# Attention: the next head's hi and lo parts in thirds over three blocks, on ScalarE and VectorE; modulation semaphores cleared

## What is computed

```python
# 8 heads, 2048 queries, 2304 keys (2048 tokens and 256 of context), q and k 96 wide, v 64 wide
def one_block(qblk):
    s = jnp.einsum('bqhd,bkhd->bhqk', qblk, k).astype(jnp.float32) * scale
    p = jax.nn.softmax(s, axis=-1).astype(v.dtype)
    return jnp.einsum('bhqk,bkhd->bqhd', p, v)
```

## Time and profile before

| | us |
|---|---|
| timed runs, median of 3 | 3417.44 (3409.56 to 3417.75) |
| the profiled execution, its own time | 3412.3 |
| its span | 3410.5 |
| TensorE busy over the span | 3076.6 (90%) |
| VectorE busy | 1947.3 (57%) |
| ScalarE busy | 1375.1 (40%) |
| GpSimd busy | 648.5 (19%) |
| attention stage, about | 1094 to 2116 |

### The profile page before, as it was taken

How to read it: one execution, slowest core, us unless ns; L and a number is a source line. 1 busy time by engine, 2 the same in 40 slices (tenths; PEclk the granted TensorE clock), 3 DMA queues, 4 the chain that set the end, 5 groups by cost and what they waited for, 6 DMA issues and landing times. The chain is left out here.

```text
span 3410.5 us, 43961 instructions
## 1 busy us (share of the span) xinstructions
PE 3076.6 (90%) x14693; PEld 2177.3 (64%) x14693; DVE 1947.3 (57%) x2632; ACT 1375.1 (40%) x2061; POOL 648.5 (19%) x459
## 2 busy tenths in 40 slices
PE   6799999999886899999999997998399999999992
PEld 1355555555586565565565563777298989989892
DVE  1133333333475677777777775444766666766663
ACT  0133333333222655666566664211244444444432
POOL 0011111111254233223322321211011111101011
PEclk9899999999877899999999998999599999999996
DMA  8521121111223110110110101332366667676656
GB/s 320 149 70 61 62 68 61 61 61 55 99 82 80 23 24 12 32 32 5 31 32 5 32 5 55 139 108 105 122 198 208 211 205 229 203 216 201 212 159 234
DMA packets 254709, 363.74 MB, mean 107 GB/s; under 512 B 36436, under 2 KB 170583, under 8 KB 252888
## 3 DMA queue, kind: packets, MB, share of 16 engines
q1 hardware_dynamic: 245336, 327.97, 30.0%
q0 software_dynamic: 9216, 33.56, 4.4%
HBM read 279.65 MB, written 81.83 MB: 106 GB/s over the span
## 5 line engine op out<-in xcount | busy, mean ns | idle before, releaser
L467 PE MATMUL bank<-w_in_sb,h_T 128*128 128x512 f32 (+1 forms) x1440 | 609.3, 578 | 2.1 <-DVE h_T L616 2.1
L1643 PE MATMUL ebank<-gathered_T,w_gate_up 128*128 128x256 f32 x4608 | 555.6, 282 | 3.5 <-DVE gathered_T L1836 1.7
L1643 PEld LDWEIGHTS ebank<-gathered_T,w_gate_up 128*128 128x128 f32 x4608 | 550.9, 189 | 7.5 <-issue 6.3
L1077 PE MATMUL abank<-scores,head_v 128*128 128x512 f32 x1152 | 546.2, 602 | 2.2 <-ACT scores L1115 2.2
L1040 PE MATMUL abank<-head_qT,head_kT 96*128 96x512 f32 x1728 | 504.8, 437 | 24.5 <-POOL head_qT L1019 24.5
L467 PEld LDWEIGHTS bank<-w_in_sb,h_T 128*128 128x128 f32 x1440 | 270.1, 191 | 299.0 <-issue 298.8
L1040 PEld LDWEIGHTS abank<-head_qT,head_kT 96*128 96x128 f32 x1728 | 327.5, 190 | 172.1 <-issue 96.1
L1103 ACT ACTIVATE scores<-abank 128x512 f32<-128x512 f32 x576 | 314.3, 608 | 77.0 <-PE abank L1040 71.2
L1077 PEld LDWEIGHTS abank<-scores,head_v 128*128 128x128 f32 x1152 | 218.3, 194 | 180.7 <-issue 163.2
L1026 POOL TENSOR_TENSOR scores<-scores,max_for_pool 128x1536 f32<-128x1536 f32 x64 | 220.9, 3474 | 571.3 <-ACT max_for_pool L1109 571.3
L1115 ACT ACTIVATE scores<-scores 128x1536 f32<-128x1536 f32 x192 | 287.4, 1498 | 40.0 <-DVE scores L1157 35.6
(11 more groups left out here) (258 smaller groups left out, 3470.2 us busy)
## 6 DMA issues: line engine op xcount, KB each, us to landing
w_gate_up_whole<-in_w_exp_gate SPq DMA_DIRECT2D x48, 1024.0 KB, 5.4
w_gate_up_whole<-in_w_exp_up SPq DMA_DIRECT2D x48, 1024.0 KB, 8.0
w_down_whole<-in_w_exp_down SPq DMA_DIRECT2D x192, 256.0 KB, 3.6
ada_w<-in_w_ada SPq DMA_DIRECT2D x12, 2048.0 KB, 12.6
scratch_ret<-ret_rows SPq DMA_DIRECT2D x72, 256.0 KB, 2.5
x_tile<-in_x_all SPq DMA_DIRECT2D x18, 512.0 KB
w_in_sb<-in_w_in SPq DMA_DIRECT2D x4, 2048.0 KB, 18.8
chunk_qk<-scratch_ret SPq DMA_DIRECT2D x16, 512.0 KB
```

The source lines that it names most:

```text
L467: m = pe.matmul(banks[bank][:, 0:n], hT[u][:, k, :], w_in[:, k, lo:lo + n], start=(k == 0), stop=(k == KD - 1))
L1077: m = pe.matmul(banks[5 + j % 2][:, :], v1[u][:, kt, :], sc[j % 2][:, kt, :], start=(kt == 0), stop=(kt == T - 1))
L1643: x = pe.matmul(banks[f % 3][:, j * CAP:(j + 1) * CAP], w_gu[c][:, wp, j, k, o:o + P], xsT[:, xp, k, :], start=(k == 0 and n == 0), stop=( ...
```

## The change

- `split_next` on ScalarE and VectorE instead of ScalarE and GpSimd. A head's 2304 key columns and 2048 query columns are cut at 768 and 1536. Piece n of both is prepared in turn n (turns 0, 1, 2) for the pair's second head and in turn 4 + n (4, 5, 6) for the next pair's first head.
- ScalarE rounds a piece of k and of q after its six groups; VectorE subtracts the same pieces after the block's output, at the end of its turn. GpSimd has no part in it.
- `rounded` and `rest` count six steps a head. `head_ready` still waits for all of them.
- Head 0 is prepared in the same thirds, all subtractions on VectorE.
- Keys and queries have one loaded-semaphore and values another. For head 0 TensorE waits for the parts alone and for values only after the first scores.
- The modulation stage allocates its semaphores itself, has GpSimd clear them at its end, and an empty block (a barrier) follows.

```diff
@@ modulation
-    with ExitStack() as ctx:
+    with stage_semaphores(nc) as sem, ExitStack() as ctx:
...
+    yield sem
+    nc.clear_and_free_semaphores(taken)
+    with nc.Block():
+        pass
@@ attention
-        kv_loaded = ParitySignal(nc, ctx, "head_kv_loaded", 4)
+        kq_loaded, v_loaded = ParitySignal(nc, ctx, "head_kq_loaded", 3), ParitySignal(nc, ctx, "head_v_loaded")
+        THIRD = TOK // 3
+        def thirds(u, n):
+
+            c = slice(n * THIRD, (n + 1) * THIRD)
+            return (kT[u], k_whole[u], c), (qT[u], q_whole[u], slice(c.start, min(c.stop, SEQ)))
+
         def split_next(split, pair, j):
 
-            if j == 1:
-                split(pair * 2 + 1, 1)
-            if j == 5 and not (isinstance(pair, int) and pair == H // 2 - 1):
-                split(pair * 2 + 2, 0)
+            if j < 3:
+                split(pair * 2 + 1, 1, j)
+            if 4 <= j < 7 and not (isinstance(pair, int) and pair == H // 2 - 1):
+                split(pair * 2 + 2, 0, j - 4)
@@ gpsimd
-            def split(head, u, parts=(0, 1)):
-
-                for n in parts:
-                    x, whole = ((kT[u], k_whole[u]), (qT[u], q_whole[u]))[n]
-                    sg["rounded"].wait(pool, head, n + 1)
-                    pool.tensor_tensor(x[:, 1, :], whole[:, 1, :], x[:, 0, :].bitcast(F32), ALU.subtract).then_inc(sg["rest"].sem, 1)
...
-                split_next(split, pair, j)
-
-            split(0, 0, parts=(1,))
@@ tensor
             def head_ready(head, u):
-                kv_loaded.wait(pe, head, u)
+                kq_loaded.wait(pe, head, u)
+                v_loaded.wait(pe, head, u)
                 sg["rounded"].wait(pe, head)
                 sg["rest"].wait(pe, head)
...
-            pe.wait_ge(ones_set, 2)
-            head_ready(0, 0)
+            sg["rounded"].wait(pe, 0)
+            sg["rest"].wait(pe, 0)
             for kt in range(T):
                 score(0, 0, 0, kt)
             max_rows(0)
             max_spread(0)
+            pe.wait_ge(ones_set, 2)
+            v_loaded.wait(pe, 0, 0)
@@ scalar
+            def split(head, u, n):
+
+                kq_loaded.wait(act, head, u)
+                for x, whole, c in thirds(u, n):
+                    act.activation(x[:, 0, c], whole[:, 1, c], ACT.Copy).then_inc(sg["rounded"].sem, 1)
@@ vector
+            def split(head, u, n):
+
+                for i, (x, whole, c) in enumerate(thirds(u, n)):
+                    sg["rounded"].wait(dve, head, 2 * n + i + 1)
+                    dve.tensor_tensor(x[:, 1, c], whole[:, 1, c], x[:, 0, c].bitcast(F32), ALU.subtract).then_inc(sg["rest"].sem, 1)
...
                 output(j, b)
-
-            sg["rounded"].wait(dve, 0, 1)
-            dve.tensor_tensor(kT[0][:, 1, :], k_whole[0][:, 1, :], kT[0][:, 0, :].bitcast(F32), ALU.subtract).then_inc(sg["rest"].sem, 1)
+                split_next(split, pair, j)
+
+            for n in range(3):
+                split(0, 0, n)
...
-ATTENTION_STEPS = {"rounded": 2, "rest": 2, "s_psum": 18, "scores": 18, "max_keys": 7, "max_T": 1, "max_rep": 2,
+ATTENTION_STEPS = {"rounded": 6, "rest": 6, "s_psum": 18, "scores": 18, "max_keys": 7, "max_T": 1, "max_rep": 2,
```

More of the change, by code:

```diff
@@ L3 @@
 from concourse import mybir
-from contextlib import ExitStack
+from contextlib import ExitStack, contextmanager
 F32 = mybir.dt.float32
@@ L116, in split_tensor, with stage_semaphores, sem @@
     return parts, whole
+@contextmanager
+def stage_semaphores(nc):
+    taken = []
+    def sem(name):
+        taken.append(nc.alloc_semaphore(name=name))
+        return taken[-1]
+    yield sem
+    nc.clear_and_free_semaphores(taken)
+    with nc.Block():
+        pass
 def mid(ap, n):
@@ L145, in modulation @@
 def modulation(nc, ins, perm, scratch, weights, w_loaded):
-    with ExitStack() as ctx:
+    with stage_semaphores(nc) as sem, ExitStack() as ctx:
         def sb(name, shape, dt=F32):
             return ctx.enter_context(nc.sbuf_tensor(name, shape, dt))
-        def sem(name):
-            return ctx.enter_context(nc.semaphore(name))
         NCH = 12
@@ L989, in load @@
             def load(head, u):
[L990 to L994, removed]
+                for dst, src, loaded in ((k_whole[u][0:NOPE, 1, :], scratch["kT_heads"][bass.ds(head, 1), :, :].rearrange("o d n -> (o d) n"), kq_loaded),
+                                 (k_whole[u][NOPE:DQ, 1, :], scratch["krT"], kq_loaded),
+                                 (q_whole[u][:, 1, :], scratch["qT"][bass.ds(head, 1), :, CTX:].rearrange("o d n -> (o d) n"), kq_loaded),
+                                 (v1[u][:, :, 0:DV], scratch["v"].rearrange("(t p) (h d) -> p t h d", p=P, h=H)[:, :, bass.ds(head, 1), :].rearrange("p t o d -> p t (o d)"), v_loaded)):
+                    sp.dma_start(dst, src).then_inc(loaded.sems[u], 32)
             load(0, 0)
```

1 line of the change is left out of this document (removed).

## The result

The changed kernel takes 3449.64 us (median of 4 runs, 3447.18 to 3456.61) against 3415.8 for the one before (4 runs). The ratio is 1.0106 with a 95% interval of 1.0085 to 1.0126: slower by 1%. The forecast was 3442 us, slower, with a range of 3416 to 3458. One of the later runs, of e3, took 4305 us at a mean granted clock of 0.69; it is in e3's median and not in any ratio.

A forecast was written before the change was run, and what follows sets the result against it. TensorE was taken as the bound. From 3412.3 us, -44.7 (splits removed), +78.5 (VectorE's pieces) and -6.5 (start) gave 3439.6; half the distance to the median made it 3442 us, range 3416 to 3458.

The forecast's parts named there:

- What goes: Attention blocks that prepare a head: without GpSimd's splits all seven surpluses of 6.39 us go, -44.7 us.
- Pieces 0 and 1: Turns 1, 2, 5, 6: VectorE's late shift makes TensorE stand some 1.54 us, twice per head, 3.08 us per head.
- nothing gives it back: Same late-shift blocks: TensorE has no idle time in the rest of the block to recover the 1.54 us.
- Piece 2: Turns 3 and 7: TensorE's first scores wait 6.39 us for head_ready, plus 1.75 us of clock; R is the reciprocal's start.
- The start: Start of the attention stage: TensorE starts near 1111.4, 6.5 us earlier, bounds 4 and 8.
- The semaphores: Clear and empty block between modulation and projection: an issue 0.3 to 1 us later is hidden, costing nothing.
- ScalarE's thirds and the loads: Attention blocks: ScalarE's some 1.6 us a block and earlier loads fit its 8 us wait, costing nothing.
- The sum: Whole kernel: 3412.3 - 44.7 + 78.5 - 6.5 = 3439.6 us, with half the distance to the median 3442 us.
- (a): Rival: the clock drops in the 1.54 us stalls as well, +12 to +25, 3454 to 3467 us; chance 0.12.
- (b): Rival: the first two pieces' stalls don't reach TensorE, the last piece's wait stays; 3421 us, no change; chance 0.11.
- (c): Rival: preparation hidden, head_ready met at turn 3; 3364 us, or 3395 with the late shifts alone; chance 0.10.
- (d): Rival: VectorE's pieces meet GpSimd's shift and wait up to 3.45 us; 3463 us at 1 us a piece; chance 0.04.

The follow-up runs named there:

- e3: Changed kernel with VectorE's first two pieces moved ahead of the shifts of groups 0 and 1, the third left behind the output: 3426.17 us, ratio 1.0019.
- e1: Changed kernel with all three VectorE pieces moved from behind the output to ahead of the shifts of groups 0 and 1: 3361.6 us, ratio 0.9825.
- e4: Kernel before the change plus only the modulation's semaphores cleared by GpSimd and the empty block: 3421.1 us, ratio 1.0008.
- e2: Changed kernel with only VectorE's last piece moved ahead of the shifts of groups 0 and 1: 3388.77 us, ratio 0.9908.
- e6: Changed kernel with heads 1 to 7 subtracted by GpSimd, in the same thirds, behind its shifts: 3453.3 us, ratio 1.0105.

## Why the prediction was right, point by point

- **What goes (45 us).** Right: the long waits for VectorE's reduction are gone from the changed kernel, and e1, with everything else in place, has thirty blocks of 875.1 us, which is 45.2 less than before. The half microsecond more is the first prepared block, which lasted 36.09 us and not 35.57.
- **Pieces 0 and 1 (21.6 us).** Measured 23.5 us in 14 blocks. The wait that I named is there with the size I gave it: the fourth score group is 1.45 us late for a shift 1.74 us late, a slack of 0.29 us against the 0.30 forecast. (The pieces took 1.74 us, not 1.84; they start 0.87 us apart.) What failed is the step "nothing gives it back". TensorE made up for 0.26 us of it by its last scores. And I followed only the path over the banks, not the one over VectorE's maxima: their reductions come the full 1.75 us late, TensorE waits 0.30 us for them in each of the 14 blocks, and the block is 1.70 us longer. So the wait of line 1051 for line 1147 isn't gone, as I had forecast, but short. That the term came out only 1.9 us too small is luck in part: the missed wait adds no more than 0.25 us a block to the one named.
- **Piece 2 (57.0 us).** Right in kind, and it was the largest term: 61.6 us, 8.80 per head. Start against start TensorE came 6.49 us late (R + 5.78 against R - 0.71; forecast 6.39). The clock was the mis-sized part: I took 1.75 us a gap from a gap of 4.47 us; it was 8.80 - 6.49 = 2.31 in the mean and 1.4 to 3.0 in single heads (37.04 to 38.67 less 29.18 and 6.49). The upper bound of 2.7 was too near.
- **The start (6.5 us).** Measured 6.6 us to the first reciprocal between the two profiles, 5.4 to 7.4 to the first scores over three profiles of before.
- **The semaphores (0).** e4: not to be told from nothing (-1.4 to +6.5 us by the interval).
- **ScalarE's thirds and the loads (0).** No wait of ScalarE for a load shows in the loop, and e1's blocks are 29.2 us with the same thirds.
- **The sum.** From retention's last transposes to the last reciprocal the forecast was +27.3 us and the profiles show +31.7: 4.6 too little for turns 3 and 7 and 1.9 for the late shifts, less the 0.5 of the first prepared block and 1.7 us given back in the last block, where the gap of 2.19 us this time did not lower the clock (1.00 over the 7 us behind it, against 0.76 in the earlier trace rows; the last block was as short in the second profile, 17.9 us). The other 6.7 us between the two profiles lie outside attention, in retention above all, which moves by more than that from one execution to the next; no term of mine stood for them. Between the medians lie 33.8 us.
- **The rivals.** (a) fell: with 14 late shifts a run the clock stayed at 1.00 in those blocks. But it wasn't tested at 1.54 us: of the 1.45 us that the group starts late, the profile, with its modelled ends of matmuls, shows 0.90 as idle time of TensorE. (b) fell: the blocks of turns 1, 2, 5 and 6 last 30.9 us, and 29.2 in e3. (c) named the right point, whether the last rest is signalled before R - 0.70: e1 and e2 put it there, and got about the times that the rival gave (3364 with nothing late, 3361.6 in e1; 3395 with the late shifts alone, 3388.8 in e2). (d) did not occur with the pieces on VectorE; no wait of a piece for GpSimd shows.

The Trainium skill's rule on which I had spent a rival (SBUF — State Buffer, Who interferes with whom) is borne out by the durations of e6, where each two-input reduction takes 2.17 us instead of 0.69 and ends only behind a subtraction of GpSimd. In the changed kernel it didn't bite: GpSimd's second shift ends at R + 3.1 to R + 3.2, as before, and the loop's pieces of 768 columns take 0.94 to 0.95 us throughout.

## What to carry to other kernels

Before work is added to an engine that shares a loop with the bound, list what the engine has queued before it and behind it, and ask who waits for each: the same 1.5 to 1.7 us of VectorE work cost 1.7 us a block in front of a shift that others awaited, 8.8 us behind an output that itself waited for TensorE, and nothing some 11 us earlier in the same turn (R - 6.8 against R + 4.0), in a gap that the trace had shown. Follow a delay along every path to the bound: here the one over ScalarE's copies was seen and the one over VectorE's maxima was not, and the second was the longer. A wait for a whole set of parts is only as early as its last part: place that one first. And when a part is late, count the gap and what TensorE's clock takes after it as two terms.

## What the runs showed of the hardware

- The price of a gap to TensorE is uneven. One of 4.47 us cost 1.75 us of clock in the kernel before (some 2.3 in the first head's block, of 36.09 us); one of 5.92 us cost 1.4 to 3.0; one of 2.72 us lowered the clock to 0.70; one of 2.19 us lowered it in the kernel before (0.76) and not in the changed one (1.00); idle times of 0.90 and 0.30 us in one block never did. The Trainium skill (TensorE: Matmul & The Clock Gate, What's actually happening) says that the gate's monitor runs freely and isn't reset when a kernel starts. That leaves room for equal gaps with different prices. It also names a spread from run to run. Of that the changed kernel's seven gaps showed nothing, to 0.05 us in two profiles; the first prepared block of the kernel before lasted 36.1 us in two profiles and 35.6 in the third. These runs don't show the monitor itself.
- Retention, with no line changed, took 190 to 205 us in the thirteen profiles, while thirty blocks of attention repeated within 0.8 us (919.7 to 920.5 in six profiles of kernels that prepare heads whole). Differences of some us between two single profiles have to be read stage by stage.
- GpSimd's two pieces, one behind the other, held up two successive VectorE reductions, one each: 4.38 us for 1.4 us of work.
